# A decoder step on one Trainium2 core: sample states in memory of their own, mixer buffers in the weight ring, the first expert's weights asked for pair by pair

## Chip, cores, metric

The kernel runs on one core of a Trainium2 chip. The metric is device time in microseconds of one execution. Before the change it is 1330.31 us, the median of three runs (1332.0, 1330.31 and 1326.93).

## What is computed

One layer of a decoder on 256 prompt tokens and 8 sample sequences of 8 tokens (320 rows of 1024, all float32). The layer norms its input, projects it once, and runs two mixers on the result: a gated delta rule with a matrix state S of 128x128 per head, and an mLSTM with a matrix memory C of 64x128 and a normaliser n of 64 per head, four heads each. The prompt starts from zero states; each sample starts from given states, and all new states are outputs. Then come an output projection, the experts, an embedding gate and a last norm:

```python
mix, new_conv, S, C, n, m = _mixers(hn, conv_st, gdn_st, c_st, n_st, m_st, w_in, ...)
x = x + mix @ w_out
top_val, top_idx = lax.top_k(logits, TOP_K)          # 4 of 32 experts
# tokens grouped by expert
hgu = xb @ w_gu[e] + b_gu[e]                         # 1024 -> 2048
gate = jnp.minimum(hgu[:, :D_FF], SWIGLU_LIMIT)
up = jnp.clip(hgu[:, D_FF:], -SWIGLU_LIMIT, SWIGLU_LIMIT)
act = (up + 1.0) * gate * jax.nn.sigmoid(SWIGLU_ALPHA * gate)
y = act @ w_down[e] + b_down[e]                      # 1024 -> 1024
x = x + gated sum of y over the token's experts
x = x + jax.nn.sigmoid(_rms(x, norm_ple_g) @ ple_gate_w) * (p @ ple_w)
```

Weights of one expert are 12 MB (8 MB for gate and up, 4 MB for down), so all 32 are 384 MB.

## The kernel before, in words

Everything is written out by hand: one instruction stream per engine, semaphores between them. All loads of weights and all stores are issued by SyncE (SP), in one queue, in the order of its code.

**The ring.** `ring` holds 12 slots of 1 MB. Two slots side by side make a pair, the unit of every load of expert weights (`load_pair`, whose DMA has line 262). Slots 0 to 7 take gate and up weights (pairs 0, 2, 4, 6), slots 8 to 11 the down weights (pairs 8, 10). The ring holds exactly one expert. Before the experts start, the mixers use the same memory: slots 8 to 11 hold the projection weights, then `wo`; slots 0 to 7 hold, one after the other, the convolution rows `xc` (later the `strips`), the activated `qkv`, the prompt states `Sp` and `Cp`, the sample state `S` (which reaches through slots 4 and 5) and the sample memory `Cs` (slots 6 and 7). Other mixer buffers (`szo`, `qm`, `kp`, `va`, `lvl`) have memory of their own.

**The experts on TensorE (PE).** `up_chunk` multiplies one slot's weights (line 1112, 8 matmuls); before an even slot it waits for that pair's DMA, after each slot it raises `w_used`. `expert(b)` runs the eight up chunks of expert b, with the gather of the next expert's rows after chunk 5 (line 1068, 12 matmuls) and their transposes after chunk 7, then the down chunks of expert b-1 (line 1123, 32 matmuls) and the transposes of the hidden row. So each expert is up(b), down(b-1). Experts 0 and 1 are written out, the other 30 are a loop.

**SP around the change.** After `wo`, SP stores the prompt states, waits for these stores (`p_stored`), then for the last read of the strips (`wqS_ps` at 2), and loads pairs 0 and 2 of expert 0. Then it stores `m_s` (8 small DMAs, line 345), loads `ptk` and `plw`, stores `S` (`gdn_s`, line 351), loads pairs 8 and 10, waits for the store of `S` and loads pair 4, loads `bdr`, stores `C` and `n` (`c_s` and `n_s`, lines 362 and 364), waits for the store of `C` and loads pair 6. Then it loads the pairs of expert 1, each when PE has used the pair's slots (`w_used`), reads the block count (line 374) and enters the loop, which reads the expert's number (line 378) and loads the four up pairs of expert b+1 and the two down pairs of expert b, each behind its `w_used`.

```python
sp.wait_ge(sem("S_stored"), 16)
for c in range(4, 6, 2):
    load_pair(sp, 0, c)
...
sp.wait_ge(sem("C_stored"), 16)
for c in range(6, 8, 2):
    load_pair(sp, 0, c)
for c in range(0, NGU, 2):
    sp.wait_ge(sem("w_used"), used(0, c + 1))
    load_pair(sp, 1, c)
```

`pw` is a set of three buffers in which ScalarE (ACT) keeps the embedding product from shortly before the experts to the end (`ple_out`, line 1478); before the change it lies on `szo` and `va`.

## Time and profile before

| what | value |
|---|---|
| median of three runs | 1330.31 us |
| the profiled execution: span, first to last instruction | 1324.3 us |
| its time beside the span | not given; the median lies 6.0 us above the span |
| PE busy | 1271.7 us, 96% |
| DVE, ACT, POOL busy | 39%, 16%, 3% |
| moved by DMA | 438.30 MB |
| mean granted TensorE clock | 0.997 of full speed |

The span counts from the first instruction to the last; every time of the trace is read from the span's start. Busy shares are means over stages that have different limits, so the forty slices, the windows and the chain of waits say more than these shares. A DMA's "us to landing" runs from its issue on SP to its last completion.

### The profile page before, as it was taken

What the parts mean: (1) busy time and instruction counts of PE and PEld (TensorE: products, weight loads), DVE (VectorE), ACT (ScalarE), POOL (GpSimd) and SP (SyncE); (2) the same over time, 40 slices, a digit from 0 to 9 for tenths busy, and PEclk for the clock granted to TensorE, in tenths of its full rate; (3) what the DMA queues carried; (4) which work ended last, traced back from release to release, by engine and by line L of the source; (5) the groups of instructions that cost most, each with busy time, mean ns of one, the idle gap of its engine ahead of it and who ended that gap; (6) DMA issues with size and microseconds to landing.
All of it is one profiled execution on the core that took longest, in us unless ns stands there. A gap on an engine that the chain in (4) does not pass through costs nothing.

```text
span 1324.3 us, 17044 instructions
## 1 busy us (share of the span) xinstructions
PE 1271.7 (96%) x6270; PEld 541.0 (41%) x6270; DVE 522.5 (39%) x1148; ACT 211.3 (16%) x421; POOL 46.3 (3%) x104
## 2 busy tenths in 40 slices
PE   6999898889899999999999999999999999999997
PEld 4764687644333333333333333333333333333333
DVE  2683444755723333433333343333334333333233
ACT  2451102142101101100110100011011000110112
POOL 5100001100000000000000000000000000000000
PEclk9999999999999999999999999999999999999999
DMA  8431110147699999999999999999999999999941
GB/s 247 122 111 64 64 65 10 67 170 283 260 430 428 429 428 429 428 429 429 430 428 429 429 428 428 429 428 430 428 429 429 428 429 429 428 430 429 428 168 40
DMA packets 56517, 438.30 MB, mean 331 GB/s; under 512 B 12586, under 2 KB 19895, under 8 KB 31882
## 3 DMA queue, kind: packets, MB, share of 16 engines
q1 hardware_dynamic: 56368, 437.89, 79.8%
q8 instruction: 18, 0.29, 0.1%
q14 instruction: 9, 0.07, 0.0%
q10 hardware_dynamic: 122, 0.04, 0.0%
HBM read 432.89 MB, written 5.02 MB: 331 GB/s over the span
## 4 chain that ended last, share of the span: by engine, by line
PE 64%; DMA 30%; DVE 3%; issue 2%; ACT 1%; POOL 0%; SPq 0%; DVEq 0%; POOLq 0%; ACTq 0%
DMA ring<-in_expert_w_gu 29%; PE bank L1112 22%; PE bank L1123 9%; PE bank L589 8%; PE bank L1098 4%; PE bank L1068 3%; PE bank L765 2%; PE bank L587 2%; PE bank L1133 1%; PE bank L1221 1%; PE bank L674 1%; PE bank L686 1%; PE bank L1076 1%; PE bank L684 1%; PE bank L1101 1%
## 5 line engine op out<-in xcount | busy, mean ns | idle before, releaser
L1112 PE MATMUL bank<-ring,SC 128*64 128x512 f32 x2048 | 477.2, 600 | 8.3 <-DMA ring<-in_expert_w_gu 3.8
L1112 PEld LDWEIGHTS bank<-ring,SC 128*64 128x64 f32 x2048 | 136.5, 137 | 297.6 <-issue 250.1
L1123 PE MATMUL bank<-ring,SC 128*64 128x512 f32 x1024 | 226.8, 595 | 0.0
L2108 DVE TENSOR_TENSOR SC<-bank,bgu 128x256 f32<-128x256 f32 x128 | 48.2, 418 | 225.2 <-PE bank L1133 225.2
L1123 PEld LDWEIGHTS bank<-ring,SC 128*64 128x64 f32 x1024 | 70.6, 137 | 133.3 <-issue 123.8
L589 PE MATMUL bank<-xT,ring 128*128 128x320 f32 x384 | 113.0, 442 | 6.6 <-ACTq L1319 5.6
L2078 DVE TENSOR_TENSOR SC<-bank,gmoe 128x512 f32<-128x512 f32 x33 | 22.8, 692 | 220.2 <-PE bank L1076 220.2
L2095 DVE TENSOR_TENSOR X<-X,bank 128x512 f32<-128x512 f32 x120 | 76.9, 683 | 50.9 <-PE bank L1098 50.9
L1487 ACT ACTIVATE SC<-bank 128x512 f32<-128x512 f32 x33 | 19.7, 597 | 460.8 <-PE bank L1068 460.8
L1068 PE MATMUL bank<-XS,SC 128*64 128x512 f32 x396 | 90.6, 592 | 0.7 <-DVE SC L2072 0.7
L2099 DVE TENSOR_TENSOR X<-X,bank 64x256 f32<-64x256 f32 x120 | 50.1, 418 | 94.6 <-PE bank L1101 92.8
L589 PEld LDWEIGHTS bank<-xT,ring 128*128 128x128 f32 x384 | 71.0, 192 | 36.1 <-ACTq L1319 7.5
L1098 PE MATMUL bank<-SC 64*128 64x512 f32 x240 | 67.7, 641 | 0.0
L1068 PEld LDWEIGHTS bank<-XS,SC 128*64 128x64 f32 x396 | 28.4, 137 | 57.5 <-issue 56.0
L1500 ACT ACTIVATE SC<-bank 128x512 f32<-128x512 f32 x31 | 18.5, 597 | 202.7 <-PE bank L1123 202.7
L1133 PEld LDWEIGHTS bank<-ident,SC 128*128 128x128 f32 x256 | 33.4, 210 | 25.9 <-issue 25.2
L445 POOL TENSOR_TENSOR nst<-nst,mhalf 128x1 f32<-128x1 f32 (+1 forms) x12 | 6.4, 541 | 1037.8 <-DVE nst L1581 1017.5
L1133 PE MATMUL bank<-ident,SC 128*128 128x128 f32 x256 | 39.4, 297 | 0.5 <-ACT SC L1492 0.5
L1098 PEld LDWEIGHTS bank<-SC 64*128 64x128 f32 x240 | 18.1, 184 | 48.7 <-issue 24.3
L1491 ACT ACTIVATE SC<-bank 128x512 f32<-128x512 f32 x32 | 19.1, 597 | 95.1 <-PE bank L1112 95.1
L765 PE MATMUL bank<-ring,xT 128*128 128x512 f32 x64 | 30.4, 605 | 1.2 <-DVE X L1596 0.8
L1504 ACT ACTIVATE SC<-SC 128x512 f32<-128x512 f32 x32 | 20.2, 630 | 60.5 <-DVE SC L2116 60.5
(480 smaller groups left out, 1014.5 us busy)
## 6 DMA issues: line engine op xcount, KB each, us to landing
ring<-in_expert_w_gu SPq DMA_DIRECT2D x128, 2048.0 KB, 23.5
ring<-in_expert_w_down SPq DMA_DIRECT2D x64, 2048.0 KB, 23.8
ring<-in_w_in SPq DMA_DIRECT2D x7, 2048.0 KB, 7.9
ring<-in_w_out SPq DMA_DIRECT2D x2, 2048.0 KB, 8.4
ring<-in_ple_gate_w SPq DMA_DIRECT2D x4, 1024.0 KB, 14.8
out_gdn_s<-ring SPq DMA_DIRECT2D x1, 2048.0 KB, 9.4
X<-in_x_prompt SPq DMA_DIRECT2D x2, 512.0 KB, 5.9
SC<-in_ple_w SPq DMA_DIRECT2D x1, 1024.0 KB, 5.4
```

The source lines that it names most:

```text
L587: ins = mm(out[0:ROWS[c], :], xT[:, k, OFF[c]:OFF[c] + ROWS[c]], w[:, k, :], start=(k == 0), stop=(k == KD - 1))
L589: ins = mm(out[:, 0:NTOK], w[:, k, c * P:c * P + P], xT[:, k, :], start=(k == 0), stop=(k == KD - 1))
L765: ins = mm(PB[0][:, :], xT[:, k, OFF[t]:OFF[t] + P], wo[:, k, 512 * n:512 * n + 512], start=(k == 0), stop=(k == KD - 1))
L1068: last = mm(PB[7][SL * h:SL * h + SL, :], SEL[:, t, :], XS[:, t, 512 * h:512 * h + 512], start=(t == 0), stop=(t == 2), skip_group_check=True)
L1098: last = mm(PB[5 + h][:, :], SELT[SL * h:SL * h + SL, P * t:P * t + P], yS[SL * h:SL * h + SL, :], start=True, stop=True)
L1112: last = mm(PB[j][SL * h:SL * h + SL, :], xg[:, c % 4, c // 4, :], w[:, FF * h + 512 * j:FF * h + 512 * j + 512], start=(c == 0), stop=(c ...
L1123: last = mm(PB[4][SL * h:SL * h + SL, :], act_t[:, 2 * (c - NGU) + kk, :], w[:, D * kk + 512 * h:D * kk + 512 * h + 512], start=(c == NGU ...
L1133: last = turn(PB[2 + m // 4][:, P * (m % 4):P * (m % 4) + P], hS[:, spread(m, 4)], ident[:, :])
L2078: tell(V.tensor_tensor(xg, PB[7][:, :].rearrange("p (j h s) -> p j h s", j=4, h=2), bc(gmoe[:, :, :].rearrange("p h j -> p j h"), 3, SL), ...
L2095: ins = V.tensor_tensor(dst, dst, PB[5 + h][0:R, :], ALU.add)
L2099: ins = V.tensor_tensor(dst, dst, PB[5 + h][64 * r:64 * r + 64, 0:256], ALU.add)
L2108: ins = V.tensor_tensor(out[:, 4 * i:4 * i + 4, :], PB[2 + i][:, :].rearrange("p (k h s) -> p k h s", k=4, h=2)[:, :, h, :], bgu[:, c0 + 4 ...
```

## The change

`S` and `Cs` leave the ring and get memory of their own (`Sf`, `Cs`). Into the ring in their place go `qm`, `kp`, `va` (tokens 0 to 255), `szo`, `lvl` and the last part of `va`, and what was there is laid out anew: slots 0 and 1 hold `qkv`; slots 2 and 3 `qm`, `kp`, `Sp`, `Cp`, two parts of `va`; slots 4 to 7 `xc` (the strips), `szo`, `lvl` and the third part of `va`. `pw` moves from `szo` and `va` onto `Sf`, so ACT waits for the store of `S` before its first `ple_out`, and SP waits for the stores of `C` and `S` only at its very end.

Expert 0's pair 0 is issued once the prompt state product and the strips are done, pair 2 after the prompt stores and the last scores of the mLSTM, pair 4 after the last read of the strips, pair 6 behind the store of `S`. The stores of `m_s`, `c_s` and `n_s` move behind the four up pairs of expert 1.

```diff
@@ -70,10 +70,9 @@
         X = sb("X", [P, 3, D])
         XS = sb("XS", [P, 3, D])
         xT = sb("xT", [P, KD, NTOK])
-        szo = sb("szo", [P, 8, NTOK])
-        qm = sb("qm", [P, H, NTOK])
-        kp = sb("kp", [P, 2, NTOK])
-        va = sb("va", [P, 3, H, DK + 1])
+        Sf = sb("Sf", [P, NSEQ * H * DK])
+        S = Sf[:, :].rearrange("p (s h v) -> p s h v", s=NSEQ, h=H)
+        Cs = sb("Cs", [P, NSEQ, 2, DK + 1])
         SC = sb("SC", [P, 15, H * P])
         ident = sb("ident", [P, P])
         ones = sb("ones", [P, P])
@@ -90,7 +89,6 @@
         inds = sb("inds", [64, NSEQ])
         inds4 = sb("inds4", [64, 4])
         lasts = sb("lasts", [64, NSEQ])
-        lvl = sb("lvl", [P, 7, P])
         iota_i = sb("iota_i", [P, SL], I32)
         iota_s = sb("iota_s", [P, SL])
         prow = sb("prow", [77, P])
@@ -142,14 +140,21 @@
             at += n
             return ring[:, at - n:at]
 
+        qkv = take(NCH * NTOK).rearrange("p (c t) -> p c t", c=NCH)
+        assert at <= 2 * SLOTW
+        at = 2 * SLOTW
+        qm = take(H * NTOK).rearrange("p (h t) -> p h t", h=H)
+        kp = take(2 * NTOK).rearrange("p (q t) -> p q t", q=2)
+        Sp = take(H * DK).rearrange("p (h v) -> p h v", h=H)
+        Cp = take(2 * (DK + 1)).rearrange("p (q v) -> p q v", q=2)
+        va = [take(H * (DK + 1)).rearrange("p (h v) -> p h v", h=H) for t in range(2)]
+        assert at <= 4 * SLOTW
+        at = 4 * SLOTW
         xcf = take(NCH * XC)
         xc = xcf.rearrange("p (c t) -> p c t", c=NCH)
-        qkv = take(NCH * NTOK).rearrange("p (c t) -> p c t", c=NCH)
-        Sp = take(H * DK).rearrange("p (h v) -> p h v", h=H)
-        Cp = take(2 * (DK + 1)).rearrange("p (q v) -> p q v", q=2)
-        S = take(NSEQ * H * DK).rearrange("p (s h v) -> p s h v", s=NSEQ, h=H)
-        assert at >= 6 * SLOTW
-        Cs = take(NSEQ * 2 * (DK + 1)).rearrange("p (s q v) -> p s q v", s=NSEQ, q=2)
+        szo = take(8 * NTOK).rearrange("p (c t) -> p c t", c=8)
+        lvl = take(7 * P).rearrange("p (l x) -> p l x", l=7)
+        va.append(take(H * (DK + 1)).rearrange("p (h v) -> p h v", h=H))
         assert at <= NGU * SLOTW
         wbuf = [ring[:, (8 + 2 * i) * SLOTW:(10 + 2 * i) * SLOTW].rearrange("p (k n) -> p k n", k=KD) for i in range(2)]
         wo = ring[:, 8 * SLOTW:12 * SLOTW].rearrange("p (k n) -> p k n", k=KD)
@@ -233,8 +238,7 @@
         lgp = scf[:, 2048:2048 + NTOK]
         ptk = scf[:, 3072:3072 + 3 * PLE].rearrange("p (t d) -> p t d", t=3)
         pT = scf[:, 3840:3840 + 2 * NTOK].rearrange("p (k t) -> p k t", k=2)
-        szf = szo[:, :, :].rearrange("p c t -> p (c t)")
-        pw = [szf[:, 0:D], szf[:, D:2 * D], va[:, :, :, :].rearrange("p t h v -> p (t h v)")[:, 0:D]]
+        pw = [Sf[:, D * t:D * t + D] for t in range(3)]
         gsc = [scf[:, 3 * D + 512 * i:3 * D + 512 * (i + 1)] for i in range(2)]
 
         x_in = [a["x_prompt"].rearrange("b t d -> (b t) d"), a["x_sample"].rearrange("b t d -> (b t) d")]
@@ -328,6 +332,9 @@
             sp.wait_ge(sem("proj"), len(PROD))
             sp.dma_start(wo[:, 0:4, :], w_out[:, 0:4, :]).then_inc(sem("wo_in"), 16)
 
+            sp.wait_ge(sem("wqS_ps"), 1)
+            sp.wait_ge(sem("strips"), 2)
+            load_pair(sp, 0, 0)
             sp.wait_ge(sem("Sp_done"), 2)
             sp.dma_start(o["gdn_p"][0, 0].rearrange("h k v -> k h v"), Sp).then_inc(sem("p_stored"), 16)
             sp.wait_ge(sem("Cp_done"), 2)
@@ -337,12 +344,10 @@
             sp.wait_ge(sem("mnew"), 2)
             sp.dma_start(o["m_p"][0], ms[0:1, 1, MNEW, :]).then_inc(sem("out"), 16)
             sp.wait_ge(sem("p_stored"), 48)
+            sp.wait_ge(sem("kb_ps"), 3)
+            load_pair(sp, 0, 2)
             sp.wait_ge(sem("wqS_ps"), 2)
-            for c in range(0, 4, 2):
-                load_pair(sp, 0, c)
-            sp.wait_ge(sem("mnew"), 3)
-            for s in range(NSEQ):
-                sp.dma_start(o["m_s"][0, s:s + 1, :], ms[LS * s:LS * s + 1, 2, MNEW, :]).then_inc(sem("out"), 16)
+            load_pair(sp, 0, 4)
             sp.wait_ge(sem("mix"), 6)
             for t in range(3):
                 sp.dma_start(ptk[0:ROWS[t], t, :], tok_dram(p_in, t)).then_inc(sem("p_in"), 16)
@@ -350,26 +355,25 @@
             sp.wait_ge(sem("Ss_done"), H)
             sp.dma_start(o["gdn_s"].rearrange("o s h k v -> k (o s h) v"), S.rearrange("p s h v -> p (s h) v"))\
                 .then_inc(sem("S_stored"), 16)
+            sp.wait_ge(sem("vx"), H + 2)
+            load_pair(sp, 0, 6)
             sp.wait_ge(sem("x1_ps"), 5)
             for c in range(NGU, NCK, 2):
                 load_pair(sp, 0, c)
-            sp.wait_ge(sem("S_stored"), 16)
-            for c in range(4, 6, 2):
-                load_pair(sp, 0, c)
             sp.wait_ge(sem("lg_part"), 2)
             sp.dma_start(bdr, a["expert_b_down"].rearrange("o e n -> (o e) n")).then_inc(sem("bdr_in"), 16)
+            for c in range(0, NGU, 2):
+                sp.wait_ge(sem("w_used"), used(0, c + 1))
+                load_pair(sp, 1, c)
+            sp.wait_ge(sem("mnew"), 3)
+            for s in range(NSEQ):
+                sp.dma_start(o["m_s"][0, s:s + 1, :], ms[LS * s:LS * s + 1, 2, MNEW, :]).then_inc(sem("out"), 16)
             sp.wait_ge(sem("Cs_done"), 3)
             sp.dma_start(o["c_s"].rearrange("o s (q h) k v -> (h k) (o s q) v", h=2),
                          Cs[:, :, :, 0:DK].rearrange("p s q v -> p (s q) v")).then_inc(sem("C_stored"), 16)
             sp.dma_start(o["n_s"].rearrange("o s (q h) (k u) -> (h k) (o s q) u", h=2, u=1),
                          nrow[:, :, :].rearrange("p s (q u) -> p (s q) u", u=1), allow_slow_non_contiguous=True)\
                 .then_inc(sem("out"), 16)
-            sp.wait_ge(sem("C_stored"), 16)
-            for c in range(6, 8, 2):
-                load_pair(sp, 0, c)
-            for c in range(0, NGU, 2):
-                sp.wait_ge(sem("w_used"), used(0, c + 1))
-                load_pair(sp, 1, c)
             sp.wait_ge(sem("routed"), ROUTED["tables"])
             rest = sp.value_load(ntot[0:1, 0:1], min_val=NE - 2, max_val=NB - 3)
             last_b = rest + 1
@@ -399,6 +403,8 @@
             for m in range(2):
                 sp.wait_ge(sem("y_ready"), 3 + m)
                 sp.dma_start(y_out[0][P:2 * P, 512 * m:512 * m + 512], X[:, 1, 512 * m:512 * m + 512]).then_inc(sem("out"), 16)
+            sp.wait_ge(sem("C_stored"), 16)
+            sp.wait_ge(sem("S_stored"), 16)
             sp.wait_ge(sem("out"), 16 * (2 + NSEQ + 4))
 
 
@@ -426,8 +432,9 @@
             fill(epsc[:, 1:2], float(DK) * EPS)
             fill(mhalf[:], -0.5)
             fill(xc[:, :, 0:CW - 1], 0.0)
-            fill(va[:, :, :, DK:DK + 1], 1.0)
-            fill(qm[:], 0.0)
+            for t in range(3):
+                fill(va[t][:, :, DK:DK + 1], 1.0)
+            fill(qm, 0.0)
             fill(g16[:], 0.0)
             fill(w16[:, :, 16:32], 0.0)
             fill(gcb[:], 0.0)
@@ -478,7 +485,7 @@
             keep(lasts[:], [[-LS, NSEQ]], -(LS - 1), 1, 1.0, ALU.not_equal)
             fill(lastr_s[:], 0.0)
             keep(lastr_s[:].rearrange("p (s i) -> p s i", s=NSEQ), [[-LS, NSEQ], [0, LS]], -(LS - 1), 1, 1.0, ALU.not_equal)
-            fill(lvl[:], 0.0)
+            fill(lvl, 0.0)
             for l in range(7):
                 s = 1 << l
                 nb = P // (2 * s)
@@ -892,7 +899,7 @@
                 pe.wait_ge(sem("sT"), t + 1)
                 pe.wait_ge(sem("mnew"), t + 1)
                 for h in range(H):
-                    last = mm(PB[4 + 3 * (h // 2)][0:R, 129 * (h % 2):129 * (h % 2) + 129], M_ST[0:R, h, 0:R], va[0:R, t, h, :],
+                    last = mm(PB[4 + 3 * (h // 2)][0:R, 129 * (h % 2):129 * (h % 2) + 129], M_ST[0:R, h, 0:R], va[t][0:R, h, :],
                               start=True, stop=True)
                 last.then_inc(sem("num_ps"), 1)
 
@@ -910,7 +917,7 @@
                 pe.wait_ge(sem("nums"), t + 1)
                 for q in range(2):
                     for hh in range(2):
-                        last = mm(PB[4][:, 129 * q:129 * q + 129], M_KW[:, 2 * q + hh, :], va[:, t, 2 * q + hh, :],
+                        last = mm(PB[4][:, 129 * q:129 * q + 129], M_KW[:, 2 * q + hh, :], va[t][:, 2 * q + hh, :],
                                   start=(hh == 0), stop=(hh == 1))
                 last.then_inc(sem("dC_ps"), 1)
 
@@ -1307,7 +1314,7 @@
                     last = A(kp[:, c - 2, :], src[:, 0:NTOK], ACT.Copy)
                 elif name == "vb":
                     R = ROWS[c]
-                    last = A(va[0:R, c, :, 0:DK], src[0:R, :].rearrange("p (h v) -> p h v", h=H), ACT.Copy)
+                    last = A(va[c][0:R, :, 0:DK], src[0:R, :].rearrange("p (h v) -> p h v", h=H), ACT.Copy)
                 elif name == "z":
                     act.wait_ge(sem("proj"), j + 1)
                     last = A(szo[:, c, :], src[:, 0:NTOK], ACT.Silu)
@@ -1477,6 +1484,7 @@
                     r0 = 64 * n if t == 2 else 0
                     A(pw[t][0:R, 512 * n:512 * n + 512], PB[PW_BANKS[t][n]][r0:r0 + R, :], ACT.Copy).then_inc(sem("pw"), 1)
 
+            act.wait_ge(sem("S_stored"), 16)
             ple_out(0)
             act.wait_ge(sem("routed"), ROUTED["larg"])
             A(t3[1][:, :, :], t3[1][:, :, :], ACT.Exp).then_inc(sem("taken"), 1)
@@ -1924,7 +1932,7 @@
             def m_spread(q):
 
                 for hh in range(2):
-                    ins = V.tensor_tensor(vexp_m[2 * q + hh][:, :, :], bc(va[0:64, 2, 2 * q + hh, 0:DK], 1, 4), bc(inds4[:, :], 2, DK), ALU.mult)
+                    ins = V.tensor_tensor(vexp_m[2 * q + hh][:, :, :], bc(va[2][0:64, 2 * q + hh, 0:DK], 1, 4), bc(inds4[:, :], 2, DK), ALU.mult)
                 tell(ins, "vx")
 
             def m_add(q):
```

What the engines compute does not change, and their order neither, except on SP. SP's queue where expert 0's first pairs are asked for, before (L262 is a load of a pair, `Sp_done` and `Cp_done` the prompt states, `wqS_ps` the products that read the strips):

```order
L327 DMA ring<-in_w_out 128x4x1024 [waits proj]
L329 DMA ring<-in_w_out 128x4x1024 [waits proj]
L332 DMA out_gdn_p<-ring 128x4x128 [waits Sp_done]
L334 DMA out_c_p<-ring 128x2x128 [waits Cp_done]
L335 DMA out_n_p<-ring 128x2x1
L338 DMA out_m_p<-ms 1x4 [waits mnew]
L262 DMA ring<-in_expert_w_gu 128x4096 [waits wqS_ps,p_stored]
L262 DMA ring<-in_expert_w_gu 128x4096
L345 DMA out_m_s<-ms 1x4 [waits mnew]
L345 DMA out_m_s<-ms 1x4 x7
```

And now (L266 is a load of a pair):

```order
L333 DMA ring<-in_w_out 128x4x1024 [waits proj]
L266 DMA ring<-in_expert_w_gu 128x4096 [waits strips,wqS_ps]
L339 DMA out_gdn_p<-ring 128x4x128 [waits Sp_done]
L341 DMA out_c_p<-ring 128x2x128 [waits Cp_done]
L342 DMA out_n_p<-ring 128x2x1
L345 DMA out_m_p<-ms 1x4 [waits mnew]
L266 DMA ring<-in_expert_w_gu 128x4096 [waits kb_ps,p_stored]
L266 DMA ring<-in_expert_w_gu 128x4096 [waits wqS_ps]
```

One pair goes ahead of the prompt stores, one waits for them and one for the strips; the eight `m_s` stores are gone from here.

SP's queue from the store of `S` to the loop, before:

```order
L351 DMA out_gdn_s<-ring 128x32x128 [waits Ss_done]
L262 DMA ring<-in_expert_w_down 128x4096 [waits x1_ps]
L262 DMA ring<-in_expert_w_down 128x4096
L262 DMA ring<-in_expert_w_gu 128x4096 [waits S_stored]
L360 DMA xT<-in_expert_b_down 32x1024 [waits lg_part]
L362 DMA out_c_s<-ring 128x16x128 [waits Cs_done]
L364 DMA out_n_s<-nrow 128x16x1
L262 DMA ring<-in_expert_w_gu 128x4096 [waits C_stored]
L262 DMA ring<-in_expert_w_gu 128x4096 [waits w_used] x4
L374 TENSOR_LOAD ntot [waits routed]
L378 TENSOR_LOAD etab
L262 ISA [waits w_used]
```

And now:

```order
L356 DMA out_gdn_s<-Sf 128x32x128 [waits Ss_done]
L266 DMA ring<-in_expert_w_gu 128x4096 [waits vx]
L266 DMA ring<-in_expert_w_down 128x4096 [waits x1_ps]
L266 DMA ring<-in_expert_w_down 128x4096
L364 DMA xT<-in_expert_b_down 32x1024 [waits lg_part]
L266 DMA ring<-in_expert_w_gu 128x4096 [waits w_used] x4
L370 DMA out_m_s<-ms 1x4 [waits mnew]
L372 DMA out_c_s<-Cs 128x16x128 [waits Cs_done]
L374 DMA out_n_s<-nrow 128x16x1
L378 TENSOR_LOAD ntot [waits routed]
L382 TENSOR_LOAD etab
L266 ISA [waits w_used]
```

Expert 1's four pairs no longer stand behind the store of `C` and behind a pair of expert 0; `m_s`, `c_s` and `n_s` now stand between them and expert 2's first pair.

## Rows read from the trace of the kernel before

**Rows 1.** The page: span, and DMA GB/s in the span's 40 equal slices

```profile
span 1324.3 us, 17044 instructions
...
GB/s 247 122 111 64 64 65 10 67 170 283 260 430 428 429 428 429 428 429 429 430 428 429 429 428 428 429 428 430 428 429 429 428 429 429 428 430 429 428 168 40
```

**Rows 2.** Chain that ended last, in order of time: start us, us, what

```profile
334.27 5.37 PE bank L1112 x24
...
345.47 20.19 DMA ring<-in_expert_w_gu
...
369.36 2.58 PE bank L1068 x12
...
772.64 2.58 PE bank L1068 x12
...
797.51 24.28 DMA ring<-in_expert_w_gu
...
1208.62 24.28 DMA ring<-in_expert_w_gu
...
1242.32 2.58 PE bank L1068 x12
```

**Rows 3.** Windows: us, PE PEld DVE ACT POOL busy (x), PEclk, DMA share, GB/s

```profile
350.20:353.60 3.40, 2.91 (x8) 1.00 (x10) 3.23 (x7) 0.00 (x0) 0.00 (x0) 0.50 1.03 443
365.00:797.00 432.00, 431.53 (x2079) 149.72 (x2077) 147.51 (x341) 49.59 (x90) 0.00 (x0) 1.00 1.01 428
797.00:1235.00 438.00, 433.96 (x2077) 149.24 (x2077) 147.82 (x343) 49.59 (x90) 0.00 (x0) 1.00 1.01 429
```

**Rows 4.** PE timeline: start us, us, engine line op out<-in xcount [idle before <-releaser]

```profile
345.26 2.75 PE L1068 MATMUL bank<-XS,SC 128*64 128x512 f32 x12
350.69 5.10 PE L1112 MATMUL bank<-ring,SC 128*64 128x512 f32 x16 [2.68 <-DMA ring<-in_expert_w_gu]
...
371.76 3.60 PE L1112 MATMUL bank<-ring,SC 128*64 128x512 f32 x16
```

**Rows 5.** SP's DMA queue in the timeline, same columns

```profile
270.54 2.36 SPq L345 DMA_DIRECT2D out_m_s<-ms  x8
...
314.10 0.33 SPq L262 DMA_DIRECT2D ring<-in_expert_w_gu  x1
...
326.04 0.39 SPq L362 DMA_DIRECT2D out_c_s<-ring  x1
326.48 4.97 SPq L364 DMA_DIRECT2D out_n_s<-nrow  x1
342.88 2.92 SPq L262 DMA_DIRECT2D ring<-in_expert_w_gu  x4
```

**Rows 6.** The same near the start: the DMA issued right behind the load of S

```profile
16.42 12.45 SPq L315 DMA_DIRECT2D ms<-in_state_mlstm_m  x1
```

**Rows 7.** DMA issues at 342.8 to 343.2 us: KB each, us to landing

```profile
ring<-in_expert_w_gu SPq DMA_DIRECT2D x1, 2048.0 KB, 7.8
```

**Rows 8.** DMA issues at 361.9 to 362.1 us, expert 2's first pair

```profile
ring<-in_expert_w_gu SPq DMA_DIRECT2D x1, 2048.0 KB, 13.4
```

**Rows 9.** DMA packets of 328.3 to 331.5 us, inside the store of c_s

```profile
DMA packets 1895, 1.04 MB, mean 325 GB/s; under 512 B 20, under 2 KB 1880, under 8 KB 1893
```

**Rows 10.** DMA packets of 331.5 to 334 us

```profile
DMA packets 2099, 0.09 MB, mean 34 GB/s; under 512 B 1946, under 2 KB 2099, under 8 KB 2099
```

**Rows 11.** DMA packets of 334 to 340 us

```profile
DMA packets 31, 0.02 MB, mean 3 GB/s; under 512 B 0, under 2 KB 31, under 8 KB 31
```

**Rows 12.** SP's lines 374 and 378: duration ns min/median/max, first and last start us

```profile
L374 SPq TENSOR_LOAD <-ntot x1: 476/476/476, 356.2 to 356.2; - x1
...
L378 SPq SEQ_ASSERT  x2: 18/18/18, 358.2 to 385.1; - x2
```

**Rows 13.** ACT timeline: the first copy into the buffer that changes place

```profile
319.07 0.60 ACT L1478 ACTIVATE szo<-bank 128x512 f32<-128x512 f32 x1 [4.23 <-PE bank L1034]
```

**Rows 14.** Issue of c_s in the page's DMA list: KB, us to landing

```profile
out_c_s<-ring SPq DMA_DIRECT2D x1, 1024.0 KB, 16.8
```

## The prediction

> **What bounds the kernel now.** I read the forty slices first. Each is 33.1 us long, and from the twelfth to the thirty-eighth, 364 to 1258 us, DMA moves 428 to 430 GB/s without a gap [rows 1]. The windows say the same of both halves of the expert stage: DMA share 1.00 and 428 to 429 GB/s, while PE is busy 431.53 of 432 us in the first half and 433.96 of 438 in the second [rows 3]. Two resources are nearly full at once, so the busy shares alone don't decide. The chain does. An expert's step from one gather (line 1068) to the next takes (772.64 - 369.36) / 14 = 28.81 us in the first half, where the chain is made of matmuls. In the second half a DMA piece of 24.28 us stands in each expert, and the step is (1208.62 - 797.51) / 14 = 29.37 us [rows 2]. A pair of 2.097 MB at 429 GB/s takes 4.89 us, six of them 29.3 us: the second step is the weights'. PE is 0.56 us an expert faster than DMA, eats up the lead with which it started, and from about 797 us on waits for weights in every expert. So what fixes expert 31's gather at 1242.32 us is when the unbroken stream of pairs began, plus its length. Behind that gather PE finishes by itself, and the tail moves with it.
>
> The stream began late. SP's issues show the store of c_s at 326.04 us and the next four pairs only from 342.88 us [rows 5]: the first of these is expert 0's pair 6, which waited for c_s to land, 16.8 us after its issue [rows 14]. PE began expert 0 at 334.27 us [rows 2] and idled 2.68 us for that pair, and the 16 matmuls behind the idle took 5.10 us instead of 3.60 [rows 4]. The granted clock of 350.2 to 353.6 us was 0.50, the 1.2 GHz level; before it fell PE had stood idle for 2.68 us [rows 3, 4].
>
> **The change, part by part.**
>
> *Expert 0's pairs.* Pair 0 goes earlier than before, pair 2 and pair 4 take the two places that pairs 0 and 2 had. Pair 6 and the two down pairs now stand behind the store of S, which had landed by 314.1 us (the issue at 314.10 had waited for it [rows 5]); three pairs of 4.9 us are in by about 329 us, before PE starts expert 0. Nobody waits for them: cost nothing, and the idle of 2.68 us and the slow matmuls go. ACT's new wait for the store of S costs nothing either: its first copy starts at 319.07 us [rows 13], 5 us behind the landing. Two more memsets on POOL lie in the first microseconds, beside the load of x. The final waits for C and S come 950 us after both have landed.
>
> *What PE gains at once.* Without waits its chunks 6 and 7 run from 345.26 + 2.75 = 348.0 to 351.6 us [rows 4]; before, they ended at 355.8. That is 4.2 us, so expert 1's gather comes at 365.2 instead of 369.36 us.
>
> *When the stream starts.* Expert 1's first pair is issued when chunk 1 of expert 0 is done: 24 matmuls take 5.37 us [rows 2], so 16 take 3.6, and the issue is at 337.9 us. A pair issued on an empty queue lands 7.8 us later [rows 7]: 345.7 us. The next slots come free at about 342, 345.4 and 351.6 us, each ahead of its turn, so the other three land at 350.6, 355.5 and 360.4 us. Before, expert 1's last up pair landed around 370.5 us, one pair ahead of expert 2's first, at 362.0 + 13.4 = 375.4 us [rows 8]. So far the stream is 10 us ahead: 5 us from the earlier issue, 4.9 us from the pair of expert 0 that left it.
>
> *What the stores take back.* m_s, c_s and n_s now stand inside the stream, where before they filled a hole. c_s is 1.05 MB in rows of 512 bytes (2,048 packets on 16 queues) and ran at 325 GB/s [rows 9], so 3.2 us: until 363.6 us. n_s is 2,048 writes of 4 bytes; 1,946 short packets passed in the 2.5 us behind c_s [rows 10], which is some 1 us as the nearest row has it (2,048 packets of c_s took 3.2 us, and these carry nothing to speak of), and 2.5 us at most. So 4 to 5 us of the 10 are gone in any case. The Trainium skill, DMA: Bandwidth & Descriptors, Specifications, has a rule that speaks against putting them here: a transfer below 512 bytes makes the engine read, modify and write. By the packets n_s costs 1 us and the sum below stands; by that rule it costs memory far longer than its packets show, and the sum would be that of the first rival. What the trace has for it is that rival's rows.
>
> *SP itself.* The issue of n_s took 4.97 us, until 331.45 us, which is where c_s's packets ran out [rows 5, 9]. The issue right behind the load of S, of the same kind of short rows, took 12.45 us [rows 6]. I read this as SP being held while the queue is full of short descriptors. Then n_s's issue ends when c_s has drained, at about 363.1 us. Behind it SP reads the block count and the first expert number, 356.2 to 358.2 us before [rows 12], which was hidden and now is not: 2.0 us, and 0.2 us for the address. Expert 2's first pair is issued at 365.3 and lands at 373.1 us instead of 375.4. **Gain 2.3 us.** Bounds: if SP is not held, m_s takes 2.36 us and n_s 4.97 us of its time [rows 5], the issue is at 361.9 and the landing at 369.7 us, gain 5.7 us; the queue itself allows no more, as n_s's packets end at 364.6. The lower bound is the first rival below. I take 2.3 because the row of the same order with short rows ahead of it [rows 6] shows the hold plainly.
>
> *The sum.* From expert 2's first pair on every pair has a free slot in time, as before, since PE also runs ahead: the whole stream is 2.3 us early. Expert 31's gather: by weights 1242.3 - 2.3 = 1240.0 us, by PE alone 365.2 + 30 x 28.81 = 1229.5 us. The later one decides. Span 1324.3 - 2.3 = 1322.0 us; with the 6.0 us between span and median, 1328.0 us. PE's own 4.2 us at expert 1 are worth nothing at the end: it only waits for weights earlier. Differences under 0.5%, 6.7 us, are about what a measurement of this kernel can't tell from none.
>
> **Rivals.**
>
> *n_s clogs the stream (slower).* After c_s's bulk had passed by 332 us, 31 packets of c_s took from 334 to 340 us [rows 11], and c_s landed only at 342.8 us [rows 5, 14], though 1.05 MB need 3.2: a few packets on one queue, as I read it, hung some 10.8 us behind the rest, right beside the 4-byte writes. In the stream that queue would hold its share of every later pair, and as the stream has no idle, it never catches up. It would end c_s at 363.6 + 10.8 = 374.4, expert 2's first pair would land at 379.3 instead of 375.4 us: 3.9 us late, 1334.2 us. It decides from a lag of 6.9 us on (363.6 + 6.9 + 4.9 = 375.4). Against it: nearly all short packets passed within 2.5 us [rows 10], so most queues weren't held, and the late ones were 31 of some 4,000. Chance 0.15.
>
> *SP is not held.* n_s's 4.97 us would be its own price. Gain 5.7 us, 1324.6 us. For it: nothing in the trace separates the two at that place. Chance 0.25.
>
> *PE becomes the bound.* If the stores cost the stream nothing, or it has slack that the windows hide, expert 31's gather comes at 1229.5 us: 12.8 us, 1317.5 us. Against it: the rates of 428 GB/s from the first slice on. Chance 0.10.
>
> *It does nothing.* The hole is only moved: DMA idles as long behind n_s as it did before pair 6, if reading the loop's numbers or the landing takes 2 us more than thought. 1330.3 us. Chance 0.05.
>
> **How the numbers follow.** The forecast has 0.45, with 1326 to 1330 as its own range. Two executions of this kernel differ by up to 5 us, so a median may be off by 1.5. The range of 1320.5 to 1334.5 us takes in SP not held, the forecast, no effect and nearly all of the clog; it leaves out PE as the bound and some noise, 0.15 to 0.2. Faster by over 0.5% (below 1323.7 us): all of PE as the bound, a quarter of the case in which SP is not held, little of the forecast, 0.17. Slower by over 0.5% (above 1337.0 us): a worse clog, 0.06. The rest is 0.77.
>
> **What would show it.** In the changed profile PE should not idle for weights in expert 0, no window near 350 us should be at 0.50 clock, and expert 1's gather should start near 365.2 us. Expert 1's first pair should be issued near 337.9 us, n_s's issue should last until c_s has drained (7 to 8 us instead of 4.97), and expert 2's first pair should be issued near 365.3 us. DMA should show a dip of 2 to 4 us around 364 us. Then 28.81 us an expert, later 29.37, the change-over near expert 18, and expert 31's gather near 1240.0 us. If n_s's issue takes 5 us, SP was not held; if expert 2's first pair lands past 375 us, the clog is real; if the step stays at 28.81 us to the end, the weights were not the bound, and the reading of the second half is wrong.

## The result, and the profile after

The changed kernel takes 1332.18 us (median of 20 runs, 1328.51 to 1339.81), the kernel before 1329.49 us (20 runs, 1325.2 to 1333.0). The ratio is 1.0034, 95% interval 1.0020 to 1.0048: slower by a third of a per cent. It lies inside the forecast range, but only because that range reaches from 9.8 us of gain to 4.2 us of loss: the forecast was a gain of 2.3 us, and the sign is wrong.

The profiled execution of the changed kernel took 1338.65 us, near the top of its runs. Executions of one kernel here differ by up to some 11 us, along with their mean granted clock (0.998 or 0.999 down to 0.990 for the changed kernel); so beside the medians I compare one distance inside the trace, and executions of like clock with each other. The page of the changed kernel, its span and DMA's rate in forty slices, where before stood [rows 1]:

```profile
span 1336.9 us, 17049 instructions
...
GB/s 244 119 112 63 63 64 8 131 168 255 239 296 429 428 428 429 427 429 429 428 428 428 428 430 427 428 430 427 429 428 428 429 426 429 430 427 429 427 172 40
```

The stream is still at 426 to 430 GB/s from the thirteenth slice on; the twelfth, 368 to 401 us, has a hole (296). Expert 0's gather, in the chain of waits of the kernel before (start us, us, what):

```profile
329.05 2.82 PE bank L1068 x12
```

and in the chain of the changed kernel, same columns, against [rows 2]:

```profile
337.55 2.82 PE bank L1075 x12
...
398.56 24.27 DMA ring<-in_expert_w_gu
...
1221.07 24.30 DMA ring<-in_expert_w_gu
...
1254.79 2.58 PE bank L1075 x12
```

Two readings. First, the span is 12.6 us longer than before, and 8.5 us of it (337.55 against 329.05) lie ahead of expert 0's gather, in the mixers. The windows of the changed kernel (us, PE, PEld, DVE, ACT, POOL busy (x), granted clock, DMA share, GB/s) show why:

```profile
269.40:272.80 3.40, 3.40 (x74) 3.40 (x68) 0.00 (x0) 0.00 (x0) 0.00 (x0) 0.50 0.96 130
317.20:327.40 10.20, 10.20 (x51) 4.05 (x49) 2.83 (x8) 1.32 (x2) 0.53 (x1) 0.50 1.02 433
```

The clock was granted at half, the 1.2 GHz level, in two stretches of 3.4 us before these (225.0 and 259.1 us) and in these two. Ahead of the first of these windows PE had stood idle for 2.17 us, until 268.6 us; ahead of the second it was busy without a gap. The stretches are not the change's: a kernel of the experiments with the old layout has the same ones at nearly the same places, and four with the new layout have none in the mixers, with expert 0's gather at 328.45 to 330.02 us.

Second, from expert 0's gather to expert 31's it is 1254.79 - 337.55 = 917.2 us, before 1242.32 - 329.05 = 913.3 us. **This stage is 4.0 us longer, and it is the change's part.** Behind it 82.1 us are left, before 82.0. The piece of weights that stood in the chain from 797.51 us on [rows 2] now stands there from 398.56 us on: from expert 3 on the chain has such a piece of 24.3 us in every expert. The forecast had the change-over near expert 18.

What PE did in expert 0 (its timeline: start us, us, engine, line, operation, xcount), against [rows 4]:

```profile
353.76 2.75 PE L1075 MATMUL bank<-XS,SC 128*64 128x512 f32 x12
356.33 3.60 PE L1119 MATMUL bank<-ring,SC 128*64 128x512 f32 x16
...
373.58 2.75 PE L1075 MATMUL bank<-XS,SC 128*64 128x512 f32 x12
```

The idle of 2.68 us is gone, the 16 matmuls take 3.60 us instead of 5.10, and expert 1's gather comes 373.75 - 337.55 = 36.2 us behind expert 0's by the chain (the timeline, whose matmul starts are a little earlier, has 373.58); before it was 369.36 - 329.05 = 40.3 us. SP's DMA queue, same columns, against [rows 5]:

```profile
346.46 13.85 SPq L266 DMA_DIRECT2D ring<-in_expert_w_gu  x4
360.35 2.35 SPq L370 DMA_DIRECT2D out_m_s<-ms  x8
362.75 0.40 SPq L372 DMA_DIRECT2D out_c_s<-Cs  x1
363.20 7.25 SPq L374 DMA_DIRECT2D out_n_s<-nrow  x1
372.84 9.06 SPq L266 DMA_DIRECT2D ring<-in_expert_w_gu  x4
```

Expert 1's pairs are asked for from 346.46 us on, 3.7 us behind PE's start of expert 0 at 342.77 us; n_s takes 7.25 us instead of 4.97 and ends at 370.45 us, when 1,003 of c_s's 2,048 rows were still to pass; expert 2's first pair is issued at 372.84 us. Its landing, in the DMA issues of that moment (last column: us from issue to landing):

```profile
ring<-in_expert_w_gu SPq DMA_DIRECT2D x1, 2048.0 KB, 14.8
```

and the windows behind it:

```profile
375.00:378.00 3.00, 3.00 (x18) 1.00 (x16) 0.00 (x0) 0.60 (x1) 0.00 (x0) 1.00 0.19 6
378.00:382.00 4.00, 4.00 (x23) 1.62 (x21) 0.99 (x3) 1.48 (x3) 0.00 (x0) 1.00 0.94 94
382.00:387.00 5.00, 5.00 (x26) 1.72 (x24) 0.46 (x3) 0.00 (x0) 0.00 (x0) 1.00 0.93 393
```

14.8 us instead of the 7.8 us of a pair on an empty queue [rows 7]. For about 3 us DMA carried 6 GB/s, then 4 us at 94 GB/s with the queues nearly full (share 0.94): the packets of these 4 us took 1.1 to 4.4 us each, where 0.6 us is usual. From 382 us on the stream was at its normal rate. Expert 1's last up pair landed at 370.55 us, expert 2's first at 387.6 us: 17.1 us between two pairs that at the stream's rate stand 4.9 us apart.

How firmly this landing fixes the end can be read from all ten profiles, those of the experiments included: expert 31's gather stands 865.9 to 867.7 us behind the landing of expert 2's first pair, whatever the kernel.

### The profile page after: what moved, and what is told of

Its sections match the earlier page's. It is cut to its first block, busy times and chain, and to the rows that moved or that the text cites. A ratio compares the mean times of both kernels' runs of the same rounds, so it can differ in the third digit from the quotient of the medians.

```text
span 1336.9 us, 17049 instructions
## 1 busy us (share of the span) xinstructions
PE 1283.6 (96%) x6270; PEld 546.1 (41%) x6270; DVE 522.3 (39%) x1148; ACT 211.6 (16%) x421; POOL 46.5 (3%) x106
## 4 chain that ended last, share of the span: by engine, by line
DMA 53%; PE 39%; DVE 4%; issue 2%; ACT 1%; POOL 0%; SPq 0%; DVEq 0%; POOLq 0%; ACTq 0%
DMA ring<-in_expert_w_gu 53%; PE bank L1119 10%; PE bank L596 8%; PE bank L1105 2%; PE bank L772 2%; PE bank L594 2%; PE bank L1130 2%; PE bank L1228 1%; PE bank L681 1%; PE bank L693 1%; PE bank L691 1%; DMA X<-in_x_sample 1%; PE bank L1075 1%; PE bank L1240 1%; PE bank L1022 1%
## 5 line engine op out<-in xcount | busy, mean ns | idle before, releaser
L1119 PE MATMUL bank<-ring,SC 128*64 128x512 f32 x2048 | 478.4, 599 | 10.1 <-DMA ring<-in_expert_w_gu 3.9
L2116 DVE TENSOR_TENSOR SC<-bank,bgu 128x256 f32<-128x256 f32 x128 | 48.1, 417 | 225.0 <-PE bank L1140 225.0
L2107 DVE TENSOR_TENSOR X<-X,bank 64x256 f32<-64x256 f32 x120 | 50.1, 418 | 99.1 <-PE bank L1108 97.4
L1105 PEld LDWEIGHTS bank<-SC 64*128 64x128 f32 x240 | 18.1, 184 | 48.7 <-DVE X L2103 24.3
## 6 DMA issues: line engine op xcount, KB each, us to landing
ring<-in_expert_w_gu SPq DMA_DIRECT2D x128, 2048.0 KB, 24.3
ring<-in_expert_w_down SPq DMA_DIRECT2D x64, 2048.0 KB, 24.3
ring<-in_ple_gate_w SPq DMA_DIRECT2D x4, 1024.0 KB, 14.9
```

Of the source, the lines that this page charges most:

```text
L1105: last = mm(PB[5 + h][:, :], SELT[SL * h:SL * h + SL, P * t:P * t + P], yS[SL * h:SL * h + SL, :], start=True, stop=True)
L1119: last = mm(PB[j][SL * h:SL * h + SL, :], xg[:, c % 4, c // 4, :], w[:, FF * h + 512 * j:FF * h + 512 * j + 512], start=(c == 0), stop=(c ...
L2107: ins = V.tensor_tensor(dst, dst, PB[5 + h][64 * r:64 * r + 64, 0:256], ALU.add)
L2116: ins = V.tensor_tensor(out[:, 4 * i:4 * i + 4, :], PB[2 + i][:, :].rearrange("p (k h s) -> p k h s", k=4, h=2)[:, :, h, :], bgu[:, c0 + 4 ...
```

## Experiments

All kernels but one start from the changed kernel. Theory A: the 4-byte writes of n_s hold the stream's reads long after their packets have been posted. Theory B: the loss is SP's, held by n_s's issue. Theory C, in the expectations, puts it into the half-clock stretches in the mixers. Times are medians; the kernel before, run beside them, took 1330.02 us in the first four and 1330.06 us in the last four. "Stage" is the distance from expert 0's gather to expert 31's, from the chain; PE alone would need 36.2 + 30 x 28.81 = 900.5 us. "Gap" is from the landing of expert 1's last up pair to that of expert 2's first. "At high clock" is the median of the executions whose mean granted clock was 0.998 or 0.999, with their number; the kernel before, whose profile has one half-clock stretch of 3.4 us in expert 0 [rows 3], reached 0.997 at most, in 8 of the 55 executions beside the experiments, and these stand there. In the diffs, a name in brackets, as (m_s, c_s, n_s), stands for the unchanged lines of these stores, and `...` for what is left out.

| kernel | median | lowest | at high clock | ratio to before, 95% | stage | gap |
|---|---|---|---|---|---|---|
| before | 1329.49 | 1325.2 | 1326.4 (8) | 1 | 913.3 | 4.9 |
| changed | 1332.18 | 1328.51 | 1329.7 (10) | 1.0034 (1.0020 to 1.0048) | 917.2 | 17.1 |
| a_tail | 1318.68 | 1317.12 | 1317.8 (5) | 0.9934 (0.9911 to 0.9957) | 904.8 | 6.0 |
| a_ns_tail | 1326.29 | 1320.15 | 1320.5 (4) | 0.9963 (0.9944 to 0.9982) | 909.6 | 9.3 |
| a_ns_rows | 1325.21 | 1321.41 | 1322.8 (6) | 0.9978 (0.9958 to 0.9998) | 910.2 | 11.3 |
| a_hole | 1325.19 | 1319.30 | 1319.3 (2) | 0.9963 (0.9944 to 0.9982) | 906.9 | 4.9 |
| b_ns_tail | 1323.42 | 1316.84 | 1317.4 (3) | 0.9945 (0.9928 to 0.9963) | 905.8 | 5.4 |
| a_cs_tail | 1330.73 | 1327.12 | 1327.6 (3) | 1.0010 (0.9992 to 1.0028) | 914.3 | 11.9 |
| a_np_tail | 1320.92 | 1314.44 | 1315.1 (2) | 0.9926 (0.9901 to 0.9952) | 905.3 | 4.9 |
| a_ns_half | 1335.41 | 1329.36 | 1329.4 (1) | 1.0051 (1.0032 to 1.0069) | 916.1 | 17.2 |

The medians mix clocks: b_ns_tail's is 4.7 us above a_tail's, but 3 of its 12 executions and 5 of a_tail's 9 ran at high clock, and those agree within 0.5 us. Stage and high clock tell the same story: from the changed kernel to a_tail they give 12.4 and 11.9 us, from the kernel before 8.5 and 8.6 us.

**a_tail: all three stores at the very end.**

```diff
                 sp.wait_ge(sem("w_used"), used(0, c + 1))
                 load_pair(sp, 1, c)
-            (m_s, c_s, n_s)
             sp.wait_ge(sem("routed"), ROUTED["tables"])
...
+            (m_s, c_s, n_s)
             sp.wait_ge(sem("y_ready"), 1)
```

> The changed kernel with its stores of m_s, c_s and n_s issued at the end, ahead of the first output store, so that nothing stands between expert 1's and expert 2's pairs. Theory A (n_s's 2,048 writes of 4 bytes hold every queue's reads for about 10 us, SP's hold lies inside that): expert 2's first pair lands 4.9 us behind expert 1's last up pair, where the changed kernel has 17.1 (370.55 to 387.66 us), so 12.2 us faster, about 1320 us in the median. Theory B (only SP's hold behind short rows costs): the same here, 7 us for the hold plus 3 us of c_s, 1322. Theory C (what is lost is in the mixers, from the half-clock stretches at 317 to 327 us): nothing, 1332.

1318.68 us. Its chain has the two gathers at

```profile
330.02 2.82 PE bank L1075 x12
...
1234.81 2.58 PE bank L1075 x12
```

and SP's queue the pairs of experts 1 and 2 in one row:

```profile
343.01 23.75 SPq L266 DMA_DIRECT2D ring<-in_expert_w_gu  x6
```

The stage falls from 917.2 to 904.8 us, 12.4 us, and the lowest run from 1328.51 to 1317.12 us, 11.4 us. So the three stores in the stream cost about 12 us, where the prediction gave them 7 to 8. At the end of the kernel, where the stream has run out, they cost nothing that shows: 82.2 us are left behind expert 31's gather, 82.0 before.

**a_ns_tail: only n_s goes to the end.**

```diff
-            sp.dma_start(o["n_s"]..., allow_slow_non_contiguous=True)
             sp.wait_ge(sem("routed"), ROUTED["tables"])
...
+            sp.dma_start(o["n_s"]..., allow_slow_non_contiguous=True)
             sp.wait_ge(sem("y_ready"), 1)
```

> The changed kernel with n_s alone issued at the end; m_s and c_s stay between expert 1 and expert 2. Theory A: c_s costs its 3.2 us and nothing else, expert 2's first pair lands about 8.1 us behind expert 1's last (17.1 before), 9 us faster, 1323 us. Theory B: SP is no longer held either, 9 us as well. A third, that any store to memory of this size inside the stream holds it: little gain, 1329 or more. Theory C: 1332.

1326.29 us, 3 us above what was expected. The stage is 909.6 us, but this execution had a half-clock stretch inside it, at 339.1 us, worth up to 1.7 us. SP issued the next pair 3.4 us behind c_s's issue instead of 10.1 us, and the gap is 9.3 instead of 17.1 us. Of the 11.1 us by which the gap of the changed kernel exceeds a_tail's, c_s with the eight small stores of m_s is 3.3 and n_s 7.8; as the bytes of c_s alone need 3.2 us, m_s costs next to nothing. The median is 7.6 us over a_tail's, more than stage (4.8) and lowest run (3.0) say; it holds more runs with half-clock stretches (4 of 12 at high clock against 5 of 9), so I go by the other two; the runs at high clock are 2.7 us apart.

**a_ns_rows: n_s in 128 rows of 64 bytes**, so that its bytes come out in another order. c_s ahead of it is as before.

```diff
-            sp.dma_start(o["n_s"].rearrange("o s (q h) (k u) -> (h k) (o s q) u", h=2, u=1),
-                         nrow[:, :, :].rearrange("p s (q u) -> p (s q) u", u=1), allow_slow_non_contiguous=True)\
-                .then_inc(sem("out"), 16)
+            sp.dma_start(o["n_s"].rearrange("o s h k -> (o s h k)").rearrange("(p x) -> p x", p=P),
+                         nrow[:, :, :].rearrange("p s q -> p (s q)")).then_inc(sem("out"), 16)
```

> The changed kernel with n_s stored at the same place as 128 rows of 64 bytes (the bytes of n_s then lie in another order). Theory A: the same as without n_s, expert 2's first pair about 8 to 9 us behind expert 1's last, 1323 us: it is the 4-byte writes and not the bytes. If any small store clogs, or if c_s itself does, the gap stays above 12 us and the time above 1328.

SP's queue:

```profile
354.13 7.19 SPq L374 DMA_DIRECT2D out_n_s<-nrow  x1
363.65 1.52 SPq L266 DMA_DIRECT2D ring<-in_expert_w_gu  x3
```

and the landing of the pair issued at 363.65 us:

```profile
ring<-in_expert_w_gu SPq DMA_DIRECT2D x1, 2048.0 KB, 9.1
```

The issue of n_s takes 7.19 us, as with 4-byte writes (7.25), though it now has 128 rows instead of 2,048 writes: it is the 2,048 rows of c_s ahead of it that hold SP. But the pair behind it lands after 9.1 us, not 14.8; with no store ahead of it the same pair takes 9.4 us in a_tail and 8.2 in a_np_tail, so these rows hold no reads at all. **Two separate costs**: SP's hold, which makes the gap 11.3 instead of 9.3 us, and the held reads, which make it 17.1. The edit changes the length of the writes and their number together; a_ns_half and a_np_tail below bear on the number. Expected were a gap of 8 to 9 us and 1323 us; SP's hold, which the expectation left out, makes it 11.3 us and 1325.21.

**a_hole: the three stores go back ahead of expert 1's pairs**, into the time in which DMA has nothing to do.

```diff
+            (m_s, c_s, n_s)
             for c in range(0, NGU, 2):
                 sp.wait_ge(sem("w_used"), used(0, c + 1))
                 load_pair(sp, 1, c)
-            (m_s, c_s, n_s)
```

> The changed kernel with the three stores back ahead of expert 1's pairs, where the kernel before had them, but without its wait for c_s and with the new layout. Theory A: the writes of n_s drain beside PE's first chunks and delay only the start of expert 1's first pair, by 0 to 4 us; expert 2's first pair lands 4.9 us behind expert 1's last; 8 to 12 us faster than the changed kernel, 1320 to 1324 us. Theory B: the hold ends before SP is needed, 12 us faster. Theory C: 1332.

SP's queue and, in a second view, the windows (columns as above):

```profile
331.12 0.40 SPq L369 DMA_DIRECT2D out_c_s<-Cs  x1
331.57 1.81 SPq L371 DMA_DIRECT2D out_n_s<-nrow  x1
343.04 27.81 SPq L266 DMA_DIRECT2D ring<-in_expert_w_gu  x7
```

```profile
338.00:340.00 2.00, 1.01 (x8) 0.58 (x8) 1.45 (x6) 0.64 (x2) 0.00 (x0) 1.00 0.00 0
342.00:344.00 2.00, 2.00 (x12) 0.82 (x10) 1.93 (x3) 0.00 (x0) 0.00 (x0) 1.00 0.00 0
344.00:346.00 2.00, 2.00 (x11) 0.54 (x9) 1.88 (x4) 0.43 (x1) 0.00 (x0) 1.00 0.05 8
346.00:348.00 2.00, 2.00 (x12) 0.72 (x10) 1.91 (x3) 0.00 (x0) 0.00 (x0) 1.00 0.64 131
350.00:352.00 2.00, 2.00 (x12) 0.63 (x10) 1.93 (x3) 0.00 (x0) 0.00 (x0) 1.00 1.02 430
```

The pair issued at 343.04 us landed after 11.0 us. The same pair, expert 1's first, took 7.9 to 8.9 us in the seven other profiles with the new layout, so 2 to 3 us are held, though the stores had moved their last bytes by 337.1 us, 5.9 us ahead of it. Nothing else loaded DMA meanwhile: the rate was zero. The stage is 906.9 us, 10.3 us better than with the stores in the stream: the median of 1325.19 us is 1.2 us above the range expected, at high clock it is 1319.3. The hold still exists, and most of it falls into idle time. One execution shows the 11.0 us.

**b_ns_tail: the kernel before, with n_s alone moved to the end.**

```diff
-            sp.dma_start(o["n_s"]..., allow_slow_non_contiguous=True)
             sp.wait_ge(sem("C_stored"), 16)
...
+            sp.dma_start(o["n_s"]..., allow_slow_non_contiguous=True)
             sp.wait_ge(sem("y_ready"), 1)
```

> The kernel before the change with one edit: the store of n_s issued at the end, ahead of the first output store. Theory A: the hole before expert 0's last pair was made by n_s too, because c_s landed 16.8 us after its issue only beside n_s's writes. Without them c_s should land some 6 us after its issue, at about 332 us, pair 6 should be issued 10 us earlier than 342.9 us, PE should not wait for it, and expert 2's first pair should land some 8 to 10 us earlier than 375.4 us: about 1320 us, nearly what the whole change reaches without the stores. Rival: c_s's landing is slow by itself, or the layout is what makes the hole; then it stays near 1330.

SP's queue, and the landing of c_s:

```profile
335.10 0.39 SPq L362 DMA_DIRECT2D out_c_s<-ring  x1
340.20 34.62 SPq L262 DMA_DIRECT2D ring<-in_expert_w_gu  x8
```

```profile
out_c_s<-ring SPq DMA_DIRECT2D x1, 1024.0 KB, 5.1
```

c_s lands after 5.1 us, where it took 16.8 [rows 14]. Not all of that difference is n_s's. Before, a pair and `bdr` stood ahead of c_s in the queue until 331.4 us, 5.3 us behind its issue; in this execution, whose mixers had half-clock stretches, they had landed before it. So 11.5 us behind the queue ahead compare with 5.1. The clean pair is a_ns_tail and the changed kernel, where c_s landed 3.1 and 9.5 us behind the last pair ahead of it. Pair 6 of expert 0 is issued at 340.20 us, before PE needs it, and the hole of the old kernel is gone without any new layout. The chain's first two gathers are 36.2 us apart here too, and the last stands at 1243.90 us:

```profile
338.11 2.82 PE bank L1068 x12
...
374.31 2.58 PE bank L1068 x12
```

```profile
1243.90 2.58 PE bank L1068 x12
```

The stage is 905.8 us, against 904.8 us of a_tail; the lowest runs are 1316.84 and 1317.12 us. The median of 1323.42 us, 3.4 us above what was expected, comes from the clock: at high clock it is 1317.4. **So the layout is worth at most 1 us** (the place of c_s and m_s differs too, and no kernel tells the two apart): expert 1's first pair waits for PE's use of slots 0 and 1 in either kernel, and the stream starts there. Its windows also show where the half-clock stretches of the changed profile belong:

```profile
270.00:273.40 3.40, 3.40 (x73) 3.40 (x68) 0.00 (x0) 0.00 (x0) 0.00 (x0) 0.50 0.04 5
317.80:328.00 10.20, 10.20 (x50) 4.05 (x48) 2.78 (x8) 1.26 (x2) 0.53 (x1) 0.50 1.00 424
```

That is the old layout, with the same 3.4 and 10.2 us at nearly the same places as in the changed kernel's windows above.

**a_cs_tail: c_s alone goes to the end, n_s stays.**

```diff
             sp.wait_ge(sem("Cs_done"), 3)
-            sp.dma_start(o["c_s"]...).then_inc(sem("C_stored"), 16)
             sp.dma_start(o["n_s"]..., allow_slow_non_contiguous=True)
...
+            sp.dma_start(o["c_s"]...).then_inc(sem("C_stored"), 16)
             sp.wait_ge(sem("y_ready"), 1)
```

> The changed kernel with c_s alone issued at the end; m_s and n_s stay between expert 1 and expert 2. Theory A (reads are held while n_s's writes drain): n_s posts 3 us earlier, and the drain of about 10 us behind it stays: expert 2's first pair lands 12 to 15 us behind expert 1's last (17.1 with c_s); 3 us faster than the changed kernel, 1329. Theory B (it was SP's hold behind c_s's rows): n_s's issue takes under 3 us instead of 7.25, SP is free early, and the gap shrinks to 6 us: 1321.

1330.73 us against 1329 by Theory A and 1321 by Theory B. SP's queue, the landing of the pair issued at 358.93 us, and DMA between 360 and 370 us in forty slices of 0.25 us:

```profile
352.19 2.36 SPq L370 DMA_DIRECT2D out_m_s<-ms  x8
354.59 0.40 SPq L372 DMA_DIRECT2D out_n_s<-nrow  x1
358.93 13.18 SPq L266 DMA_DIRECT2D ring<-in_expert_w_gu  x4
```

```profile
ring<-in_expert_w_gu SPq DMA_DIRECT2D x1, 2048.0 KB, 18.8
```

```profile
GB/s 138 9 139 3 1 2 2 1 0 0 0 0 0 0 197 197 197 66 0 66 131 66 0 0 66 66 131 0 66 66 0 0 66 66 0 0 0 66 0 0
DMA packets 2040, 0.45 MB, mean 45 GB/s; under 512 B 2013, under 2 KB 2013, under 8 KB 2013
```

n_s's issue takes 0.40 us: SP is not held at all, and expert 2's first pair is issued 29.5 us behind expert 0's gather, just as in a_tail. Still that pair lands after 18.8 us, and for 10 us DMA moves 45 GB/s, in lone packets at times. Theory B falls: 8 KB in 4-byte writes (with m_s, which costs next to nothing) cost the stage 914.3 - 904.8 = 9.5 us by themselves, and 9.8 us at high clock. The gap of 11.9 us understates it, because here expert 1's last up pair was caught as well: from the pair ahead of that one to expert 2's first it is 21.0 us, in the changed kernel 22.3.

**a_np_tail: a_tail, and n_p, the prompt's n, also at the end**, with Cp in memory of its own, so that pair 2 of expert 0 no longer waits for n_p's 256 writes.

```diff
+        Cp = sb("Cp", [P, 2, DK + 1])[:, :, :]
...
-            sp.dma_start(o["n_p"]..., allow_slow_non_contiguous=True).then_inc(sem("p_stored"), 16)
...
-            sp.wait_ge(sem("p_stored"), 48)
+            sp.wait_ge(sem("p_stored"), 32)
...
+            (m_s, c_s, n_s, n_p)
             sp.wait_ge(sem("y_ready"), 1)
```

> The kernel with all three stores at the end, and with the prompt's n_p (256 writes of 4 bytes) there too; Cp gets memory of its own for that. If 4-byte writes hold reads wherever they stand, PE's idle time of 2.2 to 2.9 us in the middle of its products with S near 265 us, which ends with a fetch of instructions that took 2 to 3.5 us instead of 1, goes away, and the wait for the prompt stores gets shorter: 2 to 3 us faster than with the three stores alone, 1316 us in the median, more if the half-clock stretches of TensorE behind that idle go with it. Rival: the idle time is the fetch's own; then no gain, 1319.

PE's timeline near 265 us in a_tail:

```profile
263.52 1.25 PE L817 MATMUL bank<-Sf,ring 128*32 128x128 f32 x34
267.70 2.84 PE L817 MATMUL bank<-Sf,ring 128*32 128x128 f32 x94 [2.92 <-issue]
```

and in a_np_tail:

```profile
262.77 3.67 PE L817 MATMUL bank<-Sf,ring 128*32 128x128 f32 x128
```

PE's stop of 2.92 us in the middle of 128 like matmuls is gone; "issue" means that nothing in the profile released it. It stands there for 2.1 to 2.9 us in all nine profiles in which n_p is stored in the mixers, the kernel before among them (263.8 to 266.7 us). The stop comes after n_p's packets, which passed from 260.1 to 260.5 us in a_tail, but before the stores that SP waited for were complete: SP issued pair 2 at 267.73 us in a_tail, 8.6 us behind n_p's issue, and in a_np_tail 1.9 us behind c_p's issue. So even 256 writes of 4 bytes, posted within half a microsecond, kept a wait for stores open for some 7 us more. The slow fetches of instructions that the expectation names are in the traces too: of the 16 KB packets between 257 and 274 us the longest took 2.1 to 3.7 us in the nine, 1.1 us here. That PE's stop ends with one is not shown. The two runs at high clock, 1314.44 and 1315.66 us, lie below all five of a_tail's (1317.12 to 1318.74), which fits that stop; the medians (1320.92 and 1318.68, 6 and 9 runs; 1316 was expected) don't show it, so the gain is not established.

**a_ns_half: n_s of sequences 0 to 3 only**, 1,024 writes; the other half isn't stored.

```diff
-            sp.dma_start(o["n_s"].rearrange(...),
-                         nrow[:, :, :].rearrange("p s (q u) -> p (s q) u", u=1), ...)
+            sp.dma_start(o["n_s"].rearrange(...)[:, 0:8, :],
+                         nrow[:, :, :].rearrange("p s (q u) -> p (s q) u", u=1)[:, 0:8, :], ...)
```

> The changed kernel with only half of n_s stored at the same place (sequences 0 to 3, 1,024 writes of 4 bytes; the other half of n_s is left out). If the hold on the reads grows with the number of writes, the gap between expert 1's last and expert 2's first pair falls from 17.1 by 3 to 5 us, and the time to about 1328. If it is a fixed time from the first such write on, the gap stays within 1 us of 17.1 and the time at 1332.

The landing of the pair behind it:

```profile
ring<-in_expert_w_gu SPq DMA_DIRECT2D x1, 2048.0 KB, 14.9
```

14.9 us with 1,024 writes, 14.8 with 2,048; gap 17.2 and 17.1 us, stage 916.1 and 917.2 us. The hold does not grow with the number of writes between these two. The median of 1335.41 us is 3 us above the changed kernel's, but six of the seven executions had a clock of 0.993 or less; the one at 0.998 took 1329.36 us, which is the changed kernel's time.

## Why the prediction was wrong, step by step

*The bound* was read rightly: the stream of weights fixes the end. Expert 2's first pair landed 46.4 us behind expert 0's gather before (375.4 - 329.05) and 50.1 us behind it after (387.6 - 337.55). That is 3.7 us late, and the stage is 4.0 us longer.

*PE's gain at once*: forecast 4.2 us, measured 40.3 - 36.2 = 4.1 us, with no idle and no half clock in expert 0. As said, worth nothing at the end.

*The start of the stream*: forecast 3.6 us behind PE's start of expert 0, measured 3.7. The last up pair of expert 1 landed 27.8 us behind that start; the forecast had 26.1.

*c_s, 3.2 us*: 3.3 us by the gaps of a_tail and a_ns_tail. Right.

*SP itself*: forecast was n_s's issue of 7 to 8 us and the next pair issued 31.0 us behind PE's start. Measured 7.25 and 30.1 us. Right in size, and the rival without a hold is out. a_ns_rows and a_cs_tail add what the forecast only assumed, that c_s's rows cause it. The end of the hold was not where the forecast put it: n_s's issue ended with 1,003 of c_s's rows still to pass, not when they had drained.

*The step that failed* is the last one of that part: "Expert 2's first pair is issued at 365.3 and lands at 373.1 us". It applied the 7.8 us of a pair on an empty queue [rows 7] right behind 2,048 4-byte writes, which I had priced at 1 us by their packets [rows 10]. The landing took 14.8 us; without these writes the same pair takes 8.2 us (a_np_tail) to 9.4 us (a_tail). The 7.0 us above the forecast, less the 0.9 us by which the issue came sooner, turn 2.3 us of gain into 3.8 us of loss, which is what the stage shows.

*The first rival* gave 3.9 us of loss and had 0.15. Its cause (n_s) was right. Its size was too, in part by luck, for its form was wrong: I read the late packets of c_s [rows 11] as one queue that hangs behind the rest. In the stream nearly all reads stalled, for 3 us at 6 GB/s and 4 us at 94. The evidence was in the rows I had: c_s landed some 10.8 us after its bulk had passed [rows 11, 14]. I argued that nearly all short packets passed within 2.5 us [rows 10]. That row tells when packets passed and not when the next read could run. And not all had passed; the kernel before has 130 more short ones from 340 to 343 us:

```profile
DMA packets 132, 0.03 MB, mean 8 GB/s; under 512 B 130, under 2 KB 130, under 8 KB 130
```

b_ns_tail shows that the same writes made the old kernel's hole.

The rule of the Trainium skill, DMA: Bandwidth & Descriptors, Specifications, which the prediction set against its own price, says that below 512 bytes the engine reads, modifies and writes. It names no time; that memory is busy longer than the packets show was my inference. The traces agree for the writes of 4 bytes (14.8 us to the next landing) and not for rows of 64 bytes, which are below 512 too (9.1 us). Why writes of 4 bytes hold the reads behind them is not shown by any run.

*The sum as measured*, in gaps: 6.0 us with no store (a_tail), 3.3 for c_s, 2.0 for SP's hold, 5.8 for the held reads: 17.1 us. The gap understates n_s: moving it out brings 7.8 us of gap, but 9.2 us at high clock (1329.7 to 1320.5). Before, the same stores stood where DMA was idle anyway, and cost a late pair in expert 0.

*Open*: why some executions grant half clock for 3.4 or 10.2 us in the mixers. PE was busy ahead of the stretch at 317 us, so idle time is no explanation there. Also open is whether c_s's own completion is caught by the writes behind it every time: behind the last load ahead of it, it landed 11.5 us later before and 9.5 in the changed kernel, but only 5.5 us after its issue on an empty queue in a_hole, where n_s stood behind it as well.

## What to carry to other kernels

Price a store of single elements by the landing of the next load behind it, not by its own packets, and put it where no load follows: 8 KB of them cost about 9.5 us of a full stream, and nothing visible at the end of the kernel. Before laying out memory anew to close a hole in a stream, look at what stands beside the late completion: moving one small store in the old kernel reached the time that the new layout reached only with all three stores at the end. Where clock and noise move the total by more than the effect, measure between two fixed events inside the stage, or compare executions of like granted clock.
